# Routed blocks of a hybrid block kernel: rank layout, fixed index count, VectorE order and the last block's transposes

## The reference, cut to what matters

```python
h = x
u = rms_norm(h, attn_norm_g)                       # 1024 tokens x 1024
proj = u @ w_in                                    # attention and linear attention, not touched by the change
h = h + concat(stick_breaking(...), gated_linear(...)) @ w_out
v = rms_norm(h, ffn_norm_g)
# routed part: each token goes to 2 of 32 experts, so 2048 (token, expert) pairs, 64 per expert on average
for each expert e, for each block of up to 128 of its tokens:
    rows = v[tokens of the block]                                 # 128 x 1024
    y    = (silu(rows @ w_gate[e]) * (rows @ w_up[e])) @ w_down[e]    # 1024x512, 1024x512, 512x1024
    out[tokens] += gate * y
```

## Time and profile before

| what | value |
|---|---|
| three runs | 1242.65, 1242.34 and 1251.41 us, median 1242.65 |
| the profiled execution: its time | 1251.64 us |
| its span on the core | 1249.3 us |
| TensorE busy with matmuls | 1182.1 us, 95% of the span |
| VectorE busy | 866.3 us, 69% |
| ScalarE busy | 734.5 us, 59% |
| GpSimd busy | 279.3 us, 22% |
| moved by DMA | 288.13 MB, mean 231 GB/s |

### The profile page before, as it was taken

The page is one execution under the profiler, slowest core; times in us unless marked ns, Lnnn a source line. Parts: engine busy times, 40 slices in busy tenths (PEclk is TensorE's granted clock), DMA queues, the critical chain, the costliest instruction groups (busy, mean ns, idle before and its releaser), DMA issues.

```text
span 1249.3 us, 17615 instructions
## 1 busy us (share of the span) xinstructions
PE 1182.1 (95%) x6164; PEld 967.4 (77%) x6164; DVE 866.3 (69%) x975; ACT 734.5 (59%) x894; POOL 279.3 (22%) x247
## 2 busy tenths in 40 slices
PE   6999999999999998999989899999999999999993
PEld 4897777877777776777878688888888878888882
DVE  5721112276556697677769889998888888889870
ACT  5532222366454593222457588877887877788770
POOL 3300000010000001233242333344434323222210
PEclk9999999999999999999979899999999999999997
DMA  8155533020000132466779999999999999999961
GB/s 260 44 198 190 173 122 110 1 68 18 18 16 19 45 133 77 146 239 255 268 248 361 331 364 375 374 375 369 373 388 376 378 370 387 370 379 385 379 229 16
DMA packets 67925, 288.13 MB, mean 231 GB/s; under 512 B 13104, under 2 KB 20289, under 8 KB 43298
## 3 DMA queue, kind: packets, MB, share of 16 engines
q1 hardware_dynamic: 51538, 238.30, 50.5%
q0 software_dynamic: 10960, 30.29, 9.0%
q10 hardware_dynamic: 5376, 18.88, 3.9%
HBM read 243.18 MB, written 48.25 MB: 233 GB/s over the span
## 4 chain that ended last, share of the span: by engine, by line
PE 31%; DMA 17%; DVE 7%; ACT 3%; issue 2%; POOL 0%; ACTq 0%; POOLq 0%; DVEq 0%
DMA raw<-in_expert_w_up 17%; PE banks L768 9%; PE banks L770 9%; PE banks L769 9%; DVE ew_l L1594 4%; ACT ew_h L1417 2%; PE banks L1109 1%; PE banks L1013 1%; PE banks L1004 1%; DVE masked L1802 1%; PE banks L937 1%; PE banks L1142 1%; PE banks L950 0%; DVE xb_l L1594 0%; PE banks L983 0%
## 5 line engine op out<-in xcount | busy, mean ns | idle before, releaser
L1594 DVE TENSOR_TENSOR ew_l<-raw,ew_h 128x2048 fp32r<-128x2048 f32 x192 | 437.4, 2290 | 59.4 <-ACT ew_h L1417 58.3
L1417 ACT ACTIVATE ew_h<-raw 128x2048 fp32r<-128x2048 f32 x192 | 368.2, 1919 | 116.8 <-PE banks L770 57.2
L768 PE MATMUL banks<-ew_h,xb_h 128*128 128x512 f32 x512 | 204.5, 399 | 7.8 <-DVE xb_l L1594 7.8
L770 PE MATMUL banks<-ew_h,xb_l 128*128 128x512 f32 x512 | 201.2, 393 | 0.0
L769 PE MATMUL banks<-ew_l,xb_h 128*128 128x512 f32 x512 | 200.8, 392 | 0.0
L1720 DVE TENSOR_TENSOR_SCAN tails<-tails 128x512 f32<-128x512 f32 (+3 forms) x96 | 94.0, 1021 | 62.7 <-ACT tails L1383 62.6
L768 PE MATMUL banks<-win_h,u_h 128*128 128x512 f32 (+1 forms) x320 | 123.2, 385 | 2.7 <-DVE u_l L1594 2.5
L768 PEld LDWEIGHTS banks<-ew_h,xb_h 128*128 128x128 f32 x512 | 97.3, 190 | 29.8 <-issue 9.4
L770 PE MATMUL banks<-win_h,u_l 128*128 128x512 f32 (+1 forms) x320 | 119.5, 373 | 0.0
L769 PE MATMUL banks<-win_l,u_h 128*128 128x512 f32 (+1 forms) x320 | 119.4, 373 | 0.0
L770 PEld LDWEIGHTS banks<-ew_h,xb_l 128*128 128x128 f32 x512 | 97.0, 189 | 20.7
(11 more groups left out here) (245 smaller groups left out, 1996.3 us busy)
## 6 DMA issues: line engine op xcount, KB each, us to landing
raw<-in_expert_w_gate SPq DMA_DIRECT2D x64, 1024.0 KB, 12.0
raw<-in_expert_w_down SPq DMA_DIRECT2D x64, 1024.0 KB, 12.8
raw<-in_expert_w_up SPq DMA_DIRECT2D x64, 1024.0 KB, 10.5
rows_dram<-zero_rows ACTq DMA_DIRECT2D x8, 2048.0 KB, 7.6
win_raw<-in_w_in SPq DMA_DIRECT2D x16, 512.0 KB, 5.2
x_in<-in_x SPq DMA_DIRECT2D x8, 512.0 KB, 9.7
raw<-in_w_out SPq DMA_DIRECT2D x4, 1024.0 KB, 5.6
h_row<-in_x SPq DMA_DIRECT2D x8, 512.0 KB, 6.6
```

The costliest lines, as they stand in the source:

```text
L768: mm(ps, lh, rh, start=start, stop=False)
L770: return mm(ps, ll, rh, start=False, stop=stop)
L1417: A(ew_h[slot % SPLIT][:, :], raw[raw_slot][:, :], ACT.Copy).then_inc(ew_h_ready, 1)
L1594: return V.tensor_tensor(dst, src, high.bitcast(fp32), SUB)
```

## The change

- **Ranks over partitions.** For experts 2 to 31, partition p now holds rank 32*(p mod 4) + p div 4. `slot` is made on VectorE at the start of the kernel from an iota and the identity; `skip_empty` computes the indices from it; the table is loaded by five DMAs in place of one.
- **Always 128 indices.** `by_size` goes, with the size classes, the load from `control` and the branches; each gather and each scatter names 128 indices.
- **Later control.** `count_blocks` and `find_extra` move behind VectorE's `step(2)` and `step(3)`; the steps 2 to 4 of the engines are written out ahead of the loop, and the engines read the number of blocks later.
- **Order of the loop.** VectorE makes `act_row` after no low part in step 2, one in steps 3 and 4 and two in the loop, in place of three everywhere, and `xb_l` one low part after it. `a_low` comes before the last two low parts. ScalarE makes `xb_h` before the fourth high part of a step.
- **Last block.** `turn_act` of the last block stands between the two halves of the down product of the block before. Its `a_h` and `a_l` are kept in `xb_h` and `xb_l`, its product goes to banks 0 and 1, its output to `y_last`, with its own `scatter_last`.

```diff
@@ constants and consts @@
-            nc.gpsimd.iota(slot[:, :], pattern=[[0, 1]], base=0, channel_multiplier=1,
+            nc.gpsimd.iota(slot_rank[:, :], pattern=[[1, P // 4], [P // 4, 4]], base=0, channel_multiplier=0,
@@ GpSimd @@
-            def by_size(i, move):
-                size = pool.value_load(control[0:1, bass.ds(i + 18, 1)], min_val=0, max_val=2)
-                with pool.If(size > 1):
-                    move(MOVED[2])
...
             def gather(i):
                 nc.gpsimd.tensor_copy(gather_idx[:, :], source[:, bass.ds(i, 1)]).then_inc(idx_ready, 1)
                 held(idx_ready, i - 3)
...
+                pool.indirect_dma_start(out=xb[:, :], out_offset=None, in_=rows_dram,
+                                        in_offset=bass.IndirectOffsetOnAxis(ap=gather_idx[:, :], axis=0),
+                                        bounds_check=EXPERTS * P + T - 1, oob_is_err=False).then_inc(rows_in, 16)
...
-            nc.gpsimd.dma_start(table[:, 0:EXPERTS, :], table_dram[0:EXPERTS * P, :].rearrange("(p e) c -> p e c", e=EXPERTS)).then_inc(
-                table_in, 16)
+            own_table = table_dram[0:EXPERTS * P, :].rearrange("(r e) c -> r e c", e=EXPERTS)
+            nc.gpsimd.dma_start(table[:, 0:2, :], own_table[:, 0:2, :]).then_inc(table_in, 16)
+            for a in range(4):
+                nc.gpsimd.dma_start(table[a:P:4, 2:EXPERTS, :], own_table[32 * a:32 * a + 32, 2:EXPERTS, :]).then_inc(table_in, 16)
...
-            for back in (3, 2, 1):
+            for back in (3, 2):
                 held(y_added, 16 * (blocks - back))
                 rows(blocks - back)
+                if back == 2:
+                    rows(blocks - 1, scatter_last)
                 held(y_ready, blocks - back + 1)
                 scatter(blocks - back)
+            held(y_ready, blocks)
+            held(y_added, 16 * (blocks - 1))
+            scatter(blocks - 1, scatter_last, y_last)
@@ TensorE @@
+                ah, al = (xb_h, xb_l) if last else (a_h, a_l)
+                y_bank = 0 if last else 5
...
-            with pe.Fori(2, blocks - 1) as i:
+            def step(i):
                 gate_up(i, (6 * i - 2, 4))
                 turn_rows(i + 1)
                 down(i - 1, (6 * i + 2, 2))
                 turn_act(i)
+
+            for i in range(2, 5):
+                step(i)
+            pe.wait_ge(control_ready, CONTROL)
+            blocks = pe.value_load(control[0:1, 0:1], min_val=0, max_val=MAX_BLOCKS - 1 - EXPERTS) + EXPERTS
+            with pe.Fori(5, blocks - 1) as i:
+                step(i)
             gate_up(blocks - 1, (6 * blocks - 8, 4))
-            down(blocks - 2, (6 * blocks - 4, 2))
+            down(blocks - 2, (6 * blocks - 4, 2), parts=(0,))
             turn_act(blocks - 1)
-            down(blocks - 1, (6 * blocks - 2, 4))
+            down(blocks - 2, (6 * blocks - 4, 2), first=True, parts=(1,))
+            down(blocks - 1, (6 * blocks - 2, 4), first=True, last=True)
@@ ScalarE, step(i, last) @@
                 if not last:
-                    for j in range(2, 4):
-                        piece(j)
+                    piece(2)
                     x_high(i + 1)
+                    piece(3)
...
+                if last:
+                    a_high(i, xb_h)
+                    back(i - 1)
+                else:
+                    back(i - 1)
+                    a_high(i)
...
-                last = A(y_row[:, HALF * b:HALF * b + HALF], bank[5 + b][:, :], ACT.Copy,
-                         scale=scatter_row[:, 1:2].bitcast(fp32))
+                last = A(y_last[:, HALF * b:HALF * b + HALF], bank[b][:, :], ACT.Copy,
+                         scale=scatter_last[:, 1:2].bitcast(fp32))
@@ VectorE @@
+            link(V.tensor_tensor(slot_rank[:, :], slot_rank[:, :], ident[:, :], MUL))
+            link(V.reduce_sum(slot[:, :], slot_rank[:, :], axis=AX.X))
...
             def skip_empty():
                 dve.wait_ge(counted, 1)
                 link(V.tensor_scalar(empty[:, :], counts, slot[:, 0:1], FAR, ALU.is_le, MUL))
-                V.tensor_tensor(source[:, 0:EXPERTS].bitcast(i32), source[:, 0:EXPERTS].bitcast(i32), empty[:, :], ADD).then_inc(
-                    control_ready, 1)
+                link(V.tensor_scalar(empty[:, :], empty[:, :], slot[:, 0:1], None, ADD))
+                V.scalar_tensor_tensor(out=source[:, 0:EXPERTS].bitcast(i32), in0=iota[:, 0:EXPERTS], scalar=float(P),
+                                       in1=empty[:, :], op0=MUL, op1=ADD).then_inc(control_ready, 1)
...
-            count_blocks()
             activate(1, 9)
...
-            low_piece(13, 13, raw_slot(13))
-            find_extra()
-            for m in (14, 15):
+            for m in (13, 14, 15):
                 low_piece(m, m, raw_slot(m))
...
+                ahead = 0 if isinstance(i, int) and i == 2 else (1 if isinstance(i, int) else 2)
                 if not last:
-                    for j in range(3):
+                    for j in range(ahead):
                         low_piece(6 * i + 4 + j, 4 + j, slot(j))
                 if last:
                     low_piece(6 * i + 4, 4, 0)
                 activate(i, 6 * i + 2)
                 if not last:
-                    low_piece(6 * i + 7, 7, slot(3))
+                    low_piece(6 * i + 4 + ahead, 4 + ahead, slot(ahead))
                     x_low(i + 1)
+                    for j in range(ahead + 1, 4):
+                        low_piece(6 * i + 4 + j, 4 + j, slot(j))
...
             step(2)
+            count_blocks()
+            step(3)
+            find_extra()
+            step(4)
             dve.wait_ge(control_ready, CONTROL)
...
-            with dve.Fori(3, blocks - 1) as i:
+            with dve.Fori(5, blocks - 1) as i:
                 step(i)
             step(blocks - 1, last=True)
```

80 lines of the change are left out of this document (34 added, 46 removed).

## The result

| | before | after |
|---|---|---|
| runs of the first comparison | 1242.34 to 1251.41 us, median 1245.99 of 4 | 1226.89 to 1229.80 us, median 1228.89 of 4 |
| ratio, 95% interval | | 0.9858 [0.9838, 0.9878] |
| a second comparison (the kernel again, 5 runs) | median 1245.52 | median 1227.92, ratio 0.9846 [0.9823, 0.9869] |
| profiled execution: its time, its span | 1251.64, 1249.3 us | 1229.80, 1228.0 us |

The change gives 17 us, 1.4%. The forecast was 1234.7 us with a range of 1225 to 1246, so the time lies inside the range but 5.8 us under the number, between the forecast's lower edge (1230.5) and rival A (1224.5 us). The gain is further off than the time: 7.9 us were forecast and 17.1 measured, more than twice as much.

The account below looks back on a forecast made before the run. TensorE's pace was taken to bound the kernel, with transfers pacing some stretches. 1251.64 - 5.0 (start) + 2.1 (loop) - 5.0 (end) = 1243.7 us profiled; the same 7.9 us off the median gives 1234.7, range 1225 to 1246.

Parts of the forecast that it names:

- the forecast's lower edge: Whole run: lower end of the forecast's own band, 1230.5 to 1236.5 us, which was given a chance of 0.43.
- rival A: Loop: its waits vanish too, the start's 5.0 us stays and up to 8.1 more: 1224.5 us; chance 0.22.
- The start: First blocks: fewer TensorE waits for `act_row` and `xb_l`; 5.0 us gained, ends 3.3 and 5.7.
- walk: Start: new order followed with the profile's durations; `gate_up(4)` starts at 712.4 us in place of 718.1, 5.7 us sooner.
- The ends of 3.3 to 5.7: Start: bounds of its gain in us; a clock falling behind the 1.9 us idle would take another 1.7.
- The end: Last block: 5.0 us gained, 4.0 on TensorE (2.24 idle, 1.7 clock) and 1.0 without size load and branches.
- a wait of 0.1: End: the last scatter waits for the scatter before to land, late next, at a cost of 0.1 us.
- The loop: Loop: transfers set the later blocks' pace again, 2.9 us of the start's lead kept, 2.1 lost; ends 4.3 loss, 8.1 gain.
- The two that were set against each other: Loop: skipped indices cost 0.27 us a block, spreading earns 0.28; taken as 0, ends +37 and -8.1 us.
- B: Whole run: only the end is won, the start's lead is spent in the loop: 1237.6 us; chance 0.21.
- C: Loop: skipped indices cost DMA engines 0.17 us each, 1.0 us a block, so slower: 1262 us; chance 0.14.

Follow-up runs that it names:

- e3_old_order: Changed kernel with ScalarE's and VectorE's order of a step undone, the rest kept: 1235.52 us, ratio 0.9919 to the kernel before.
- e4_end_only: Kernel before with the last block's new end alone; size classes and branches stay: 1242.88 us, ratio 0.9980.
- e6_128_contiguous: Kernel before with 128 indices always and the later control, rank r still on partition r, old order and end: 1260.08 us, ratio 1.0117.
- e1_contiguous: Changed kernel with the layout alone undone, rank r on partition r again, 128 indices kept: 1252.41 us, ratio 1.0052 to the kernel before.
- e2: Kernel before with the spread ranks, the 128 indices and the later control alone, old order and end: 1238.06 us, ratio 0.9948.
- e10: Changed kernel with ranks 0 to 31 on partitions 0 to 31, 32 to 63 on 64 to 95, 64 to 95 on 32 to 63: 1231.50 us.
- e13: Changed kernel in the layout of e10, with 96 indices in place of 128 in every gather and scatter: 1243.14 us, ratio 0.9985 to the kernel before.
- e7_order_only: Kernel before with ScalarE's and VectorE's new order of a step alone, old layout, size classes and end: 1244.93 us, ratio 0.9987.
- e8_more_skipped: Changed kernel with one more gather of 128 skipped indices in each of 28 blocks: 1227.64 us, ratio 0.9850 to the kernel before.

## Why the prediction was right and wrong

**The start: right in mechanism, 1.2 us small.** Gain 6.2 us, forecast 5.0 (walk 5.7). The walk put `gate_up(4)` at 712.4 behind a single idle of 1.9; measured are 709.94 and 1.57, and without the 2.0 us by which the whole kernel is earlier there, 711.9. The ends of 3.3 to 5.7 were meant for a clock that falls behind that idle. It did not: the granted clock is 1.00. `e3_old_order` takes 5.1 us of the gain back.

**The end: right, 0.7 us small.** Forecast 4.0 on TensorE, 1.0 for the branches and a wait of 0.1; the traces have 4.05, 1.0 and 0.4. Another 1.0 us went behind the issue of the last scatter (14.2 to 13.2 us), a term that the sum did not have and that stays open. The median of `e4_end_only` gives 2.5 for the new end alone, where its trace has 3.2, and of the 4.0 on TensorE the 1.7 for the clock are not there in each kernel.

**The loop: the step that failed.** The forecast has "a loss of 2.1", because "with a share of 1.01 the transfers then set the pace of the later blocks again". The share was read as a fixed capacity: 16 engines busy, nothing to spare, so the same bytes take the same time. It is no such thing. The changed kernel has the share of 1.01 at 386 GB/s, `e6_128_contiguous` 1.00 at 366, `e1_contiguous` 0.97 at 368. (At equal bytes per block the GB/s only say again how long a block takes; what counts is that the share hardly moves with it, while gate and down pieces land after 7.8 and 7.3 us in the changed kernel, after 12.0 and 12.8 in the kernel before, and after 14.1 and 14.0 in `e6_128_contiguous`.) How long the transfers of a block take hangs on how its rows lie, as `e1`, `e2` and `e10` to `e13` show; that it is the fullest engine and the crowded half that a block waits for fits the table and is shown by no row of a single engine. The gain of 7.6 us is the earlier trace rows going away, and with it the lead of the start is kept; the two together are 9.7 us from the term. The prediction also read the earlier trace rows alone: over the same stretch the kernel before waits 12.8 us for gate pieces and 3.7 for down pieces too, so not only what stood behind the up pieces was late, and `e7_order_only` shows what freeing `xb_l` from them does by itself.

**The two that were set against each other.** The forecast took 128 indices (+0.27 us a block at 0.045 each) and the spreading (-0.28) as zero. Skipped indices cost nothing (`e8_more_skipped`). The spreading is worth 0.42 us a block, together with the fixed 128, against the old layout at the old sizes (`e7_order_only` to the changed kernel) and 0.79 against the old layout at 128 indices (`e1_contiguous`). The difference of 0.5% between two stretches of the earlier trace rows, from which I read 0.045 us, was none that skipped indices made: it was 2 GB/s between two stretches of one kernel, and too little to hang a price on. For the spreading I priced the fullest engine (0.28 us), which is part of it, and not the half of the partitions.

**The rule of the Trainium skill.** The prediction took from "DMA: Bandwidth & Descriptors" that a DMA over 128 partitions gives each engine two groups of four, and that an expert with 64 tokens has four rows per engine before and after. That holds by the map, and the sum was said to be as taken. But I had left out where the two groups lie. With the whole rule, the 128 indices in the old layout would have been seen to put eight rows on each of eight engines, which `e6_128_contiguous` times at 12.9 us over the kernel before: the spreading is what makes the fixed 128 possible, not an extra beside it.

**Rivals.** A had 0.22. Counted as a gain its 18.1 us are the nearest to the measured 17.1. It is what happened in the loop, for half of its reason: `xb_l` freed from the second up piece did nothing alone (`e7_order_only`: 0.1%), and the spreading did it. The order earns its part only with the layout: 1.6 us alone, 6.6 us on top of it (`e3_old_order`). B is out. C is out as a price of the skipped index.
